# Attention scores of a stick-breaking encoder step: two full-height passes in place of three half-height ones

## The reference, cut to what matters

```python
p = rmsnorm(x) @ w_in                # [GLU a | GLU b | q | k | v | gate_conv | gate_attn]
glu = p_a * sigmoid(p_b)             # -> causal depthwise conv, 31 taps -> LayerNorm -> silu -> @ w_pw2
z = einsum('bqhd,bkhd->bhqk', q, k) * 64 ** -0.5
log_1m = where(mask, log_sigmoid(-z), 0)                  # mask: key position < query position
tail = reverse_cumsum(log_1m) - log_1m
a = where(mask, exp(log_sigmoid(z) + tail), 0);  attn = a @ v
x += (sigmoid(gate_conv) * conv_out + sigmoid(gate_attn) * attn) @ w_out
x += relu(rmsnorm(x) @ w_up) ** 2 @ w_down                # final rmsnorm on the outputs
```

## Time and profile before

| | before |
|---|---|
| median of 3 runs | 1058.3 us (1057.99 to 1060.88) |
| profiled execution, its own time | 1058.21 us |
| span of its instructions | 1056.5 us |
| PE busy | 1031.9 us (98%) |
| DVE busy | 570.2 us (54%) |
| ACT busy | 460.5 us (44%) |
| POOL busy | 345.9 us (33%) |
| mean granted clock of TensorE | 0.961 of full |

### The profile page before, as it was taken

One profiled execution on the slowest core, in us unless ns is written; L12 is line 12 of the kernel. 1 busy time (PEld: TensorE's weight loads), 2 busy tenths in 40 slices (PEclk: granted clock), 3 DMA queues, 4 the chain that ended last, 5 costly groups with the idle time before them and its releaser, 6 DMA issues.

```text
span 1056.5 us, 19811 instructions
## 1 busy us (share of the span) xinstructions
PE 1031.9 (98%) x7761; PEld 993.0 (94%) x7761; DVE 570.2 (54%) x821; ACT 460.5 (44%) x722; POOL 345.9 (33%) x171
## 2 busy tenths in 40 slices
PE   7999989999999999999999999999999999999996
PEld 6899888989999899989999999999999999999995
DVE  3459796888979797878967433222211112221122
ACT  4365563545455554646466243443311123341133
POOL 4423230223213222223332433434443423344230
PEclk8998998999998989998999999999999999999998
DMA  6221312221131313230421323232423222324202
GB/s 189 83 72 33 101 52 80 60 82 51 43 109 32 100 40 92 60 87 0 130 90 53 99 84 97 81 99 79 119 80 95 85 61 83 96 80 120 60 20 85
DMA packets 157745, 83.55 MB, mean 79 GB/s; under 512 B 3696, under 2 KB 156544, under 8 KB 157709
## 3 DMA queue, kind: packets, MB, share of 16 engines
q1 hardware_dynamic: 147261, 78.21, 25.4%
q10 hardware_dynamic: 10448, 4.84, 1.6%
HBM read 75.97 MB, written 7.06 MB: 79 GB/s over the span
## 4 chain that ended last, share of the span: by engine, by line
PE 91%; DVE 3%; issue 2%; ACT 1%; SPq 1%; DMA 1%; POOL 0%; ACTq 0%; DVEq 0%
PE dense L414 77%; PE z L500 4%; PE z L472 4%; PE pv L530 2%; PE z L467 1%; PE z L475 1%; PE dense L540 1%; DMA w_raw<-in_w_in_dram 1%; DVE acc L1071 1%; DVE n L1052 1%; SPq L297 1%; DVE sum_sq L1211 0%; POOL r_lo L395 0%; DVE yconv L1206 0%; SPq L278 0%
## 5 line engine op out<-in xcount | busy, mean ns | idle before, releaser
L389 POOL TENSOR_TENSOR w_lo<-w_raw,w_hi 128x1024 fp32r<-128x1024 f32 x136 | 335.0, 2466 | 674.0 <-ACT w_hi L718 674.0
L414 PE MATMUL dense<-r_hi,w_hi 128*128 128x272 f32 (+1 forms) x1280 | 280.2, 301 | 3.9 <-DVE kT L1149 3.6
L414 PE MATMUL dense<-r_lo,w_hi 128*128 128x272 f32 (+1 forms) x1280 | 274.3, 297 | 0.0
L414 PE MATMUL dense<-r_hi,w_lo 128*128 128x272 f32 (+1 forms) x1280 | 274.0, 296 | 0.0
L1071 DVE SCALAR_TENSOR_TENSOR acc<-conv_in,cw_cur,acc 128x574 f32<-128x574 f32 x232 | 221.8, 1011 | 0.0
L414 PEld LDWEIGHTS dense<-r_hi,w_hi 128*128 128x128 f32 x1280 | 211.3, 198 | 5.1 <-issue 2.9
L414 PEld LDWEIGHTS dense<-r_lo,w_hi 128*128 128x128 f32 x1280 | 210.5, 196 | 0.0
L414 PEld LDWEIGHTS dense<-r_hi,w_lo 128*128 128x128 f32 x1280 | 210.3, 196 | 0.0
L718 ACT ACTIVATE w_hi<-w_raw 128x1024 fp32r<-128x1024 f32 x136 | 142.6, 1051 | 153.9 <-PE dense L414 137.2
L414 PE MATMUL dense<-s_lo,w_hi 128*128 128x272 f32 x640 | 132.4, 288 | 0.0
L414 PE MATMUL dense<-s_hi,w_hi 128*128 128x272 f32 x640 | 132.3, 288 | 0.0
(11 more groups left out here) (246 smaller groups left out, 1238.7 us busy)
## 6 DMA issues: line engine op xcount, KB each, us to landing
w_raw<-in_w_in_dram SPq DMA_DIRECT2D x56, 512.0 KB, 3.9
w_raw<-in_w_up_dram SPq DMA_DIRECT2D x32, 512.0 KB, 4.0
w_raw<-in_w_down_dram SPq DMA_DIRECT2D x32, 512.0 KB, 3.6
w_raw<-in_w_pw_dram SPq DMA_DIRECT2D x8, 512.0 KB, 3.6
w_raw<-in_w_out_dram SPq DMA_DIRECT2D x8, 512.0 KB, 3.6
out_dram<-v_tok ACTq DMA_DIRECT2D x8, 256.0 KB, 2.3
out_dram<-k_tok ACTq DMA_DIRECT2D x8, 256.0 KB, 2.3
out_dram<-y_tok SPq DMA_DIRECT2D x4, 512.0 KB, 3.9
```

Of the source, the lines that this page charges most:

```text
L389: pool.tensor_tensor(w_lo[:, s], w_raw[:, s], w_hi[:, s].bitcast(F32), ALU.subtract).then_inc(lo_done, 1)
L414: mm = nc.tensor.matmul(dense[:, slot, h, 0:half], w[:, wslot, k, :], m[:, k, c0 + h * half:c0 + (h + 1) * half], start=(k == 0 and n == 0 ...
```

## The change

A head's operands are laid out over all 128 rows. `k_both[:, hh]` holds k's high part in the head's own 64 rows and the low part in the other 64. `q_twice[:, hh]` holds q's high part in both halves; `q_low[:, hh]` holds q's low part in the head's own rows and zeros in the others. Then `q_twice` x `k_both` is high x high + high x low in one pass, and `q_low` x `k_both` is the third product. `q_end` holds the last 48 query columns (the ones that the plain float32 scores use) with zeros in the other head's rows.

```diff
                 def score(bank, off, keys, q0, q1, start=False):
-                    return nc.tensor.matmul(z[:, bank, off:off + q1 - q0], keys, qT[r, q0:q1], start=start, stop=False, skip_group_check=True)
+                    return nc.tensor.matmul(z[:, bank, off:off + q1 - q0], keys, q_end[:, hh, q0 - SEQ + META:q1 - SEQ + META], start=start, stop=False, skip_group_check=True)
 
                 def score_split(bank, off, j, q0, start=False):
-                    for n, (kp, qp) in enumerate(((k_hi, q_hi), (k_hi, q_lo), (k_lo, q_hi))):
-                        nc.tensor.matmul(z[:, bank, off:off + SEQ - q0], kp[r, j * P:(j + 1) * P], qp[r, q0:SEQ], start=(start and n == 0), stop=False, skip_group_check=True)
+                    for n, qp in enumerate((q_twice, q_low)):
+                        nc.tensor.matmul(z[:, bank, off:off + SEQ - q0], k_both[:, hh, j * P:(j + 1) * P], qp[:, hh, q0:SEQ], start=(start and n == 0), stop=False, skip_group_check=True)
...
                 act.wait_ge(tile_done, tile(i, T_Q) + 1)
-                nc.scalar.activation(cols2(q_hi[:], HALFO), psum2(0, HALFO), ACT.Copy, scale=HD ** -0.5)
-                nc.scalar.activation(cols2(qT[:], HALFO), psum2(0, HALFO), ACT.Copy, scale=HD ** -0.5).then_inc(qhi_done, 1)
+                for hh, r in enumerate(HEAD_ROWS):
+                    nc.scalar.activation(q_end[r, hh, :], dense[r, 0, 1, HALFO - META - DEC:HALFO], ACT.Copy, scale=HD ** -0.5)
+                for hh, r in enumerate(HEAD_ROWS):
+                    nc.scalar.activation(cols2(q_twice[r, hh, :], HALFO), dense[r, 0, :, 0:HALFO], ACT.Copy, scale=HD ** -0.5).then_inc(qhi_done, 1)
                 if not first:
                     high_ahead(3)
                 act.wait_ge(tile_done, tile(i, T_K) + 1)
-                nc.scalar.activation(cols2(k_hi[:], HALF), psum2(1, HALF), ACT.Copy).then_inc(khi_done, 1)
+                for hh, r in enumerate(HEAD_ROWS):
+                    nc.scalar.activation(cols2(k_both[r, hh, :], HALF), dense[r, 1, :, 0:HALF], ACT.Copy).then_inc(khi_done, 1)
...
                     probabilities(2 * i - 1, 1)
+                act.wait_ge(qhi_done, 2 * i + 2)
+                for hh, (r, other) in enumerate(zip(HEAD_ROWS, reversed(HEAD_ROWS))):
+                    mm = nc.scalar.activation(q_twice[other, hh, :], q_twice[r, hh, :].bitcast(F32), ACT.Copy)
+                mm.then_inc(q_doubled, 1)
                 high_ahead(5)
...
-                dve.wait_ge(qhi_done, i + 1)
-                nc.vector.scalar_tensor_tensor(cols2(q_lo[:], HALFO), psum2(0, HALFO), HD ** -0.5, cols2(q_hi[:].bitcast(F32), HALFO), ALU.mult, ALU.subtract).then_inc(q_kept, 1)
+                if first:
+                    dve.wait_ge(tile_done, tile(i, T_Q) + 1)
+                    for hh, other in enumerate(reversed(HEAD_ROWS)):
+                        nc.vector.tensor_copy(q_low[other, hh, :], sum_y[other, :])
+                        nc.vector.memset(q_end[other, hh, :], 0.0)
+                for hh, r in enumerate(HEAD_ROWS):
+                    dve.wait_ge(qhi_done, 2 * i + 1 + hh)
+                    mm = nc.vector.scalar_tensor_tensor(cols2(q_low[r, hh, :], HALFO), dense[r, 0, :, 0:HALFO], HD ** -0.5, cols2(q_twice[r, hh, :].bitcast(F32), HALFO), ALU.mult, ALU.subtract)
+                mm.then_inc(q_kept, 1)
                 conv_before(4)
-                dve.wait_ge(khi_done, i + 1)
-                nc.vector.tensor_tensor(cols2(k_lo[:], HALF), psum2(1, HALF), cols2(k_hi[:].bitcast(F32), HALF), ALU.subtract)
+                dve.wait_ge(khi_done, 2 * i + 2)
+                for hh, (r, other) in enumerate(zip(HEAD_ROWS, reversed(HEAD_ROWS))):
+                    nc.vector.tensor_tensor(cols2(k_both[other, hh, :], HALF), dense[r, 1, :, 0:HALF], cols2(k_both[r, hh, :].bitcast(F32), HALF), ALU.subtract)
```

More of the change, by code:

```diff
@@ L119, in build @@
         rstd_tok = sb("rstd_tok", [P, 5])
-        rstd = sb("rstd", [P, TOK])
         keys = ExitStack()
-        k_hi = sb("k_hi", [P, TOK], F32R, where=keys)
-        k_lo = sb("k_lo", [P, TOK], F32R, where=keys)
+        k_both = sb("k_both", [P, 2, TOK], F32R, where=keys)
+        q_low = sb("q_low", [P, 2, OUTTOK], F32R, where=keys)
         keys.close()
         n32 = sb("n32", [P, 2, TOK])
+        rstd = sb("rstd", [P, TOK])
+        sum_sq = sb("sum_sq", [P, OUTTOK])
+        HEAD_ROWS = (slice(0, HD), slice(HD, P))
         sq = n32[:].rearrange("p a c -> p (a c)")[:, 0:D]
@@ L159, in build @@
         start.close()
-        qT = sb("qT", [P, OUTTOK], where=loop)
+        q_end = sb("q_end", [P, 2, META + DEC], where=loop)
         ckT = sb("ckT", [P, 2 * P], where=loop)
@@ L182, in build @@
         gate_a = sb("gate_a", [P, OUTTOK], where=loop)
-        q_hi = sb("q_hi", [P, OUTTOK], F32R, where=loop)
-        q_lo = sb("q_lo", [P, OUTTOK], F32R, where=loop)
+        q_twice = sb("q_twice", [P, 2, OUTTOK], F32R, where=loop)
         loop.close()
@@ L191, in build @@
         part = sb("part", [P, 2, OUTTOK], where=post)
-        sum_sq = sb("sum_sq", [P, OUTTOK], where=post)
         rows_back = ExitStack()
@@ L222, in build @@
         r_ready_pool, qhi_done, khi_done = sem("r_ready_pool"), sem("qhi_done"), sem("khi_done")
+        q_doubled = sem("q_doubled")
         a_kept, gb_abs, gb_exp, gb_ln, gb_log, gb_done = (sem(n) for n in ("a_kept", "gb_abs", "gb_exp", "gb_ln", "gb_log", "gb_done"))
@@ L457, in scores @@
             def scores(i, hh, first=False):
-                r = slice(hh * HD, (hh + 1) * HD)
                 if hh == 0:
@@ L464, in scores @@
                     pe.wait_ge(k_kept, i + 1)
+                    pe.wait_ge(q_doubled, i + 1)
                 def score(bank, off, keys, q0, q1, start=False):
-                    return nc.tensor.matmul(z[:, bank, off:off + q1 - q0], keys, qT[r, q0:q1], start=start, stop=False, skip_group_check=True)
+                    return nc.tensor.matmul(z[:, bank, off:off + q1 - q0], keys, q_end[:, hh, q0 - SEQ + META:q1 - SEQ + META], start=start, stop=False, skip_group_check=True)
                 def score_split(bank, off, j, q0, start=False):
-                    for n, (kp, qp) in enumerate(((k_hi, q_hi), (k_hi, q_lo), (k_lo, q_hi))):
-                        nc.tensor.matmul(z[:, bank, off:off + SEQ - q0], kp[r, j * P:(j + 1) * P], qp[r, q0:SEQ], start=(start and n == 0), stop=False, skip_group_check=True)
+                    for n, qp in enumerate((q_twice, q_low)):
+                        nc.tensor.matmul(z[:, bank, off:off + SEQ - q0], k_both[:, hh, j * P:(j + 1) * P], qp[:, hh, q0:SEQ], start=(start and n == 0), stop=False, skip_group_check=True)
                 def mask(bank, off, m):
                     return nc.tensor.matmul(z[:, bank, off:off + m.shape[1]], ident_b[:], m, start=False, stop=False, skip_group_check=True)
-                score(*S_CACHE0, ckT[r, 0:P], SEQ, OUTTOK, start=True)
-                score(*S_CACHE1, ckT[r, P:2 * P], SEQ, OUTTOK)
+                score(*S_CACHE0, ckT[:, 0:P], SEQ, OUTTOK, start=True)
+                score(*S_CACHE1, ckT[:, P:2 * P], SEQ, OUTTOK)
                 score_split(0, 0, 0, 0, start=True)
@@ L490, in scores @@
                 mask(bank, off, neg_diag[:])
-                score(*LAST, kT[r, 4 * P:5 * P], SEQ - META, OUTTOK)
+                score(*LAST, kT[:, 4 * P:5 * P], SEQ - META, OUTTOK)
                 mask(*LAST, neg_last[:]).then_inc(z_scored, 1)
```

## The result

| | before | after |
|---|---|---|
| median, in the same comparison | 1058.23 us (1057.99 to 1060.88, 4 runs) | 1066.89 us (1065.71 to 1068.20, 4 runs) |
| span | 1056.5 us | 1064.3 us |
| PE busy | 1031.9 us | 997.1 us |
| DVE busy | 570.2 us | 587.7 us |
| mean granted clock | 0.961 | 0.967 |

What follows compares the result with a forecast made beforehand. TensorE was taken as the bound at 98% busy, with VectorE only 1.1 us behind in the stretch up to unit 2. Seven turns +1.8, first turn -0.3, behind the loop -2.1: together -0.6, 1057.6 us, range 1045 to 1068.

Steps and rivals of the forecast that it cites:

- A, 31.98 + 1.3 = 33.3 us: Loop stretch from unit 4 to the next turn's unit 2: turn 2's 31.98 us plus VectorE's additions of 1.3.
- together 1.3 us: VectorE ahead of the copy of k: one more q_lo (0.64) and k_lo (0.65) operation in each turn.
- B, 26.4 us: Loop stretch from unit 2 to the end of unit 4: 26.4 us, with no clock fall behind the new `scores`.
- 7.96 (unit 2 as in turn 2): Unit 2's 48 matmuls at the low clock behind TensorE's wait: 7.96 us instead of 6.26.
- The first turn, -0.3: First turn: 1.3 us more until k is freed, 1.6 less in its first `scores`.
- Behind the loop, -2.1: After the loop: the last shorter `scores` gains at most VectorE's 2.09 us wait for TensorE's mean.
- the 1.6 forecast: TensorE's `scores`: 2.7 us instead of 4.27, a gain of 1.6 us for each of 16 heads.
- the clock still falls behind the first head's scores: Slower rival in the loop: 1.5 us a turn for the clock's fall, 7 times, 1068 us; chance 0.13.
- the breaks stay: Slower rival in `scores`: breaks between matmuls keep costing 1.0 us in eight `scores`, 1065.5 us; chance 0.12.
- GpSimd's second operation misses the taps: Faster rival, from unit 4 to the next turn's unit 2: 2.1 us less, 7 times, 1043 us; chance 0.08.
- the clock does not fall in the wait: Faster rival at unit 2: no or only a brief fall, up to 1.7 us a turn, 1046 us; chance 0.15.
- The change does what it says: Faster rival: TensorE stays the bound and 16 x 1.6 = 26 us are gained, near 1015 us; chance 0.05.

Runs made afterwards that it cites:

- one_head_lows: The changed kernel, with VectorE making only the second head's low parts of q and k from the second turn on; 1057.62 us, ratio 1.0004.
- fill: The changed kernel, with 18 further matmuls of 512 columns, their result overwritten, in TensorE's wait for k; 1050.80 us, ratio 0.9933.
- both_late: The changed kernel, with ScalarE's rounding of the weights of units 3 and 4 moved behind the doubling of q; 1022.29 us, ratio 0.9665.
- high4_late: The changed kernel, with ScalarE's rounding of unit 4's weights moved behind the doubling of q; 1045.76 us, ratio 0.989.

## Why the prediction was right or wrong

The forecast was 1057.6 us, no change, with 0.46 for it. It came out 8.7 us slower than before, inside the range of 1045 to 1068, but not the way that was forecast. The mechanism held: VectorE's list bounds A, and the low clock at unit 2 comes behind the wait. Two terms of the sum were too small. By the terms:

- **A, 31.98 + 1.3 = 33.3 us: mechanism right, size off by 0.5.** The wait for L1168, both GpSimd operations in the taps, the same length in every turn: all as said. The step that failed is "together 1.3 us": I took 0.64 and 0.65 for each added operation. The pairs cost 0.85 (1.49 - 0.64) and 0.86 more than the single operations, together 1.71. Of this the added operations are 1.48 (`one_head_lows`), and 0.23 is that an operation of 64 rows lets the next begin later. The other 0.18 lie in the start of A. I took 126.14 from the chain; in the timeline, by which the A of the changed kernel is cut, unit 4 of turn 2 ends at 125.96, so that A was 32.16 us. From q's low part to kT's copy VectorE took 7.58 us in it and takes 9.24 now, and 32.16 + 1.66 = 33.82 is what was measured (33.83). Over seven turns +3.7 us.
- **B, 26.4 us: off by 0.5.** The step that failed is "7.96 (unit 2 as in turn 2)". Behind the waits of 4.7 us unit 2 takes 7.70 to 9.10 us in the seven turns, 8.67 on average, +0.7; turn 2 was one sample, behind a wait of 2.7. `scores` took 2.48 instead of 2.7, -0.2. Over seven turns +3.6 us. What the low clock costs in all was shown by `fill`, where unit 2 takes 6.35.
- **The first turn, -0.3: nearly right.** Unit 2 starts 1.17 later (43.85), and its B takes 23.47 us, 1.25 less by the same view, together -0.1.
- **Behind the loop, -2.1: half of it, and that by luck.** From the last end of unit 4 the rest takes 571.76 us, 1.2 less by the same view. The step that failed is that I took VectorE's whole wait for the mean as gained by the shorter last `scores`. TensorE did come earlier, but then waited 2.91 us for GpSimd's low weights (four operations L391 took 16.45 us there, 11.88 before) and ran the unit at a clock of 0.78. So up to the mean only 0.3 was gained. The other 0.9 lie between the mean and the end, in parts that the change does not touch; where, was not followed.
- The misses add up to 3.7 + 3.6 + 0.2 + 0.9 = 8.4 us, which is what lies between the forecast (-0.6) and the spans (+7.8).

What was said of `scores` held: 1.70 us less a head against the 1.6 forecast, no breaks, no fall behind them. The Trainium skill ("TensorE: Matmul & The Clock Gate", Part 3) says that a weight load overlaps matmuls in flight only when it goes to other row groups; the same part elsewhere lets one into the background weight buffer pass too. The flat rule doesn't agree with the trace, in which the load of all 128 rows for the second pass starts beside the first pass:

```profile
174.00 0.48 PE L476 MATMUL z<-q_twice,k_both 128*128 128x512 f32 x1
174.09 0.19 PEld L476 LDWEIGHTS z<-q_low,k_both 128*128 128x128 f32 x1
```

Of the rivals, "the clock still falls behind the first head's scores", "the breaks stay", "GpSimd's second operation misses the taps" and "the clock does not fall in the wait" are refuted by the trace. "The change does what it says", given 0.05, was refused by VectorE for the reason given, and `both_late` shows what it is worth once VectorE is freed. What I had not weighed was that the errors of the two terms, each within the 0.6 us that I had allowed, could point the same way in all seven turns.

That the GpSimd operations slow the taps fits the Trainium skill ("SBUF — State Buffer", on its two sides), by which VectorE with two SBUF inputs and GpSimd exclude each other for whole instructions. The trace agrees. The first tap ends 0.62 us behind the first GpSimd operation (216.74 and 216.12), the second 0.62 behind the second (219.58 and 218.96), and in between, while the first tap ran on, GpSimd's second operation stood longer: 2.83 us, where its first took 2.39.

## What to carry to other kernels

Before a change that takes work from the busiest engine, ask in each stretch which engine is next and by how much it is behind: here 98% busy hid that VectorE was 1.1 us from being the bound, and the change also gave VectorE work. When an engine gets faster, look at what it releases earlier, since work on other engines (here ScalarE's weight rounding, then GpSimd) moves with it and may meet the very operations that it waits for. A wait of TensorE can cost more than its length, because the clock may be lower behind it: in the changed kernel those of 4.7 us did, in `both_late` those of 0.7 and 1.3 did not (unit 2 in 6.35 to 6.38 us).

## What was not expected of the hardware

- How long TensorE stays at 1.2 GHz behind a wait varies at one length of the wait: 48 matmuls took 7.70 to 9.10 us behind seven waits of 4.7 us (8.67 on average), 7.88 to 7.92 behind six of 2.58 and 6.33 behind a seventh (`high4_late`), and 6.33 to 6.39 at the full clock. Filling the waits with matmuls nobody needs made the kernel 16 us faster.
- The granted clock falls behind `scores` of 64 rows, with no wait ahead of it, and does not behind those of 128 rows, with two passes or three; whether height, breaks or length decides is open.
- Halving the rows of a VectorE operation gives nothing: one of 64 rows lasts 0.73 us, one of 128 lasted 0.72. The next begins after 0.76 us behind 64 rows and after 0.64 behind 128, so the split costs 0.85, more than the whole operation did.
